# A one-core transformer kernel: paced first transfers, two weight slabs by halves, five matmuls ahead, and a last norm divided anew between engines

## The reference, cut to what matters

```python
def first_block(x, g_mix, w_in, ...):
    h = _rmsnorm(x, g_mix[layer])
    proj = jnp.einsum('bsd,de->bse', h, w_in[layer])     # 1024 -> 3072
    ...
def second_block(x, ..., final_norm):
    ...
        h = h + swiglu(rmsnorm(h, ffn_norm[l]), w_gate[l], w_up[l], w_down[l])
    return rmsnorm(h, final_norm)

def rmsnorm(x, g):
    xf = x.astype(jnp.float32)
    inv = lax.rsqrt(jnp.mean(xf * xf, axis=-1, keepdims=True) + RMS_EPS)
    return (xf * inv).astype(x.dtype) * g
```

## Time and profile before

| What | Value |
|---|---|
| Median of three runs | 1027.2 us (1026.72 to 1028.21) |
| The profiled execution's own time | 1030.3 us |
| Its span, first to last instruction | 1028.6 us |
| PE busy | 1009.0 us, 98% |
| DVE, ACT, POOL busy | 707.9, 603.1, 54.7 us |
| First matmul starts | 9.07 us |
| Last matmul ends | 1021.37 us |
| Granted TensorE clock, mean | 0.997 |

### The profile page before, as it was taken

The page is one execution under the profiler, slowest core; times in us unless marked ns, Lnnn a source line. Parts: engine busy times, 40 slices in busy tenths (PEclk is TensorE's granted clock), DMA queues, the critical chain, the costliest instruction groups (busy, mean ns, idle before and its releaser), DMA issues.

```text
span 1028.6 us, 19877 instructions
## 1 busy us (share of the span) xinstructions
PE 1009.0 (98%) x7312; PEld 937.1 (91%) x7312; DVE 707.9 (69%) x1342; ACT 603.1 (59%) x1070; POOL 54.7 (5%) x76
## 2 busy tenths in 40 slices
PE   6999999999999999999999999999999999999997
PEld 6999899999999999999999999999999899999996
DVE  4645887786666668666496666668877686666664
ACT  5566786475555556555475555558655675555554
POOL 2022000030000002000020000002100020000000
PEclk9999999999999999999999999999999999999999
DMA  8643344455555554333545555554653445555531
GB/s 329 222 144 124 123 145 164 165 185 184 184 184 184 186 187 170 126 129 124 164 152 188 185 186 185 186 184 164 209 171 114 126 150 194 185 184 184 184 123 41
DMA packets 49208, 172.74 MB, mean 168 GB/s; under 512 B 5376, under 2 KB 7680, under 8 KB 49024
## 3 DMA queue, kind: packets, MB, share of 16 engines
q1 hardware_dynamic: 48096, 170.93, 50.9%
q10 hardware_dynamic: 1056, 1.05, 0.5%
HBM read 169.86 MB, written 1.05 MB: 166 GB/s over the span
## 4 chain that ended last, share of the span: by engine, by line
PE 90%; DVE 7%; ACT 2%; DMA 1%; issue 0%; POOLq 0%; SPq 0%; POOL 0%; ACTq 0%; DVEq 0%
PE bank L319 88%; DVE w_lo L1195 2%; DVE a_pair L1207 2%; PE bank L506 1%; DVE xT L1224 1%; DMA xT<-xT_dram 1%; DVE arena_r L1207 1%; ACT w_hi L814 0%; DVE tmp L1188 0%; DVE arena L1188 0%; ACT a_pair L854 0%; ACT L1027 0%; DVE arena L1498 0%; ACT soft_p L904 0%; DVE tmp L1393 0%
## 5 line engine op out<-in xcount | busy, mean ns | idle before, releaser
L319 PE MATMUL bank<-a_pair,w_hi 128*128 128x256 f32 (+1 forms) x1992 | 541.3, 344 | 9.5 <-ACT a_pair L1041 9.1
L319 PE MATMUL bank<-a_pair,w_lo 128*128 128x256 f32 x1488 | 418.2, 282 | 0.0
L814 ACT ACTIVATE w_hi<-stage 128x1024 fp32r<-128x1024 f32 x319 | 335.5, 1056 | 137.5 <-PE bank L319 132.7
L1195 DVE TENSOR_TENSOR w_lo<-stage,w_hi 128x1024 fp32r<-128x1024 f32 x319 | 390.0, 1230 | 10.5 <-ACT w_hi L814 10.3
L319 PEld LDWEIGHTS bank<-a_pair,w_hi 128*128 128x128 f32 x1992 | 344.6, 191 | 57.6 <-issue 12.6
L319 PE MATMUL bank<-arena_r,w_hi 128*128 128x256 f32 x1840 | 338.1, 285 | 1.1 <-DVE arena_r L1207 0.7
L319 PEld LDWEIGHTS bank<-arena_r,w_hi 128*128 128x128 f32 x1840 | 286.0, 191 | 5.5 <-DVE arena_r L1195 1.3
L319 PEld LDWEIGHTS bank<-a_pair,w_lo 128*128 128x128 f32 x1488 | 283.8, 191 | 0.0
L319 PE MATMUL bank<-arena_r,w_lo 128*128 128x256 f32 x920 | 259.4, 283 | 0.0
L319 PEld LDWEIGHTS bank<-arena_r,w_lo 128*128 128x128 f32 x920 | 175.5, 191 | 0.0
L1369 DVE TENSOR_TENSOR tmp<-bank,arena 128x256 f32<-128x256 f32 x123 | 51.6, 420 | 160.5 <-ACT arena L980 160.5
(11 more groups left out here) (148 smaller groups left out, 635.1 us busy)
## 6 DMA issues: line engine op xcount, KB each, us to landing
stage<-slab_dram SPq DMA_DIRECT2D x319, 512.0 KB, 4.0
con<-con_dram SPq DMA_DIRECT2D x1, 1153.5 KB, 11.6
xT<-xT_dram SPq DMA_DIRECT2D x4, 256.0 KB, 6.9
arena<-arena ACTq DMA_DIRECT2D x2, 512.0 KB, 7.3
out_dram<-arena SPq DMA_DIRECT2D x8, 128.0 KB, 2.0
vec<-vec_dram SPq DMA_DIRECT2D x1, 245.5 KB, 3.9
pos<-pos_dram SPq DMA_DIRECT2D x1, 128.0 KB, 11.5
```

The lines of the kernel that those rows point to most:

```text
L319: return nc.tensor.matmul(out, lhsT, rhs, start=start, stop=True, skip_group_check=True)
L814: nc.scalar.activation(w_hi[:, slot, :], stage[:, slot, :], ACT.Copy).then_inc(hi_made, 1)
L1195: return nc.vector.tensor_tensor(out, a, hi.bitcast(f32), ALU.subtract)
```

## The change

At the start SP issues first halves, quarters and gains, and waits between them for earlier ones to land; slabs 0 and 1 come, are split and are multiplied in halves; `vec` is cut in two, the gains (128 x 64) early and the rest behind `con`; five float32 matmuls on a tile that POOL has set to zero stand ahead of the first product on PE; the lambda work on DVE keeps its place behind `w_lo` of slab 3 and waits for the second part of `vec`; `norm_sum(0)` and what follows from it stand one slab later. At the end DVE adds the squares of chunks 0 to 4 into one tile (four additions), so that PE has four float32 matmuls and not eight; DVE makes six of the eight chunks times gain, ACT two; DVE multiplies by `rB` in four pairs of chunks; three transfers carry a pair each, and the last pair goes as two chunks, one from SP and one from ACT. POOL has no part in it.

```diff
+HALF = SLAB // 2
+WARM = 5
...
@@ sync
-            for n in range(SLOTS):
+            half_in(0, False)
+            x_in(0)
+            sp.dma_start(vec[:, 0:V_BGATE], vec_d[:, 0:V_BGATE]).then_inc(in_gain, 16)
+            x_in(1)
+            sp.wait_ge(in_half[0], 16)
+            half_in(0, True)
+            x_in(2)
+            sp.wait_ge(in_x[0], 16)
+            x_in(3)
+            sp.wait_ge(in_x[1], 16)
+            half_in(1, False)
+            half_in(1, True)
+            sp.wait_ge(in_x[2], 16)
+            first_load(2)
+            sp.wait_ge(in_x[3], 16)
+            first_load(3)
+            sp.wait_ge(loaded[1], 16)
+            first_load(4)
+            first_load(5)
+            sp.dma_start(con[:, :], con_d).then_inc(in_con, 16)
+            sp.dma_start(vec[:, V_BGATE:], vec_d[:, V_BGATE:]).then_inc(in_vec, 16)
+            sp.dma_start(pos[:, :], pos_d).then_inc(in_pos, 16)
...
-            for c in range(NC):
-                if c in POOL_CHUNKS:
-                    sp.wait_ge(pout_ready, POOL_CHUNKS.index(c) + 1)
...
+            for c in (0, 2, 4):
+                sp.wait_ge(out_ready, c // 2 + 1)
+                sp.dma_start(out_d[:, c:c + 2, :], outT[:, c:c + 2, :]).then_inc(out_done, 16)
+            sp.wait_ge(out_ready, 4)
+            sp.dma_start(out_d[:, 6, :], outT[:, 6, :]).then_inc(out_done, 16)
@@ tensor
+            pe.wait_ge(warm_ready, 1)
+            for _ in range(WARM):
+                mm(half(7, 0), soft_t[:, 0, 0:P], soft_t[:, 0, 0:TOK], True)
...
-                    if n == 3:
+                    if n == 4:
                         norm_sum(0)
...
-            for c in range(NC):
+            pe.wait_ge(ff_made, 22 * 3)
+            pe.wait_ge(fin_added, 4)
+            mm(half(7, 0), ones, sumsq[:, :], True)
+            for c in (5, 6, 7):
                 pe.wait_ge(fin_squared, c + 1)
...
+                last = mm(half(7, 0), ones, squared[:, c, :], False)
@@ scalar
+            half_split_hi(0, False)
+            act.wait_ge(in_gain, 16)
             for c in range(NC):
                 if c % 2 == 0:
                     act.wait_ge(in_x[c // 2], 16)
                 nc.scalar.activation(a_hi[:, c, :], xT[:, c, :], ACT.Copy, scale=gain(0, c)).then_inc(ahi_ready, 1)
-            for n, cs in ((1, (0, 1)), (2, (2, 3, 4)), (3, (5, 6, 7)), (4, ()), (5, ())):
+                if c == 3:
+                    half_split_hi(0, True)
+            half_split_hi(1, False)
+            half_split_hi(1, True)
+            for n, cs in ((2, (0, 1, 2)), (3, (3, 4)), (4, (5, 6)), (5, (7,))):
                 split_hi(n, n, 0)
                 squares(0, cs)
...
+            norm_end(6)
+            act.wait_ge(out_ready, 4)
+            nc.scalar.dma_start(out_d[:, NC - 1, :], outT[:, NC - 1, :]).then_inc(out_done, 16)
@@ vector
+            half_split_lo(0, False)
+            for c in range(NC):
+                dve.wait_ge(ahi_ready, c + 1)
+                scaled_lo(a_lo[:, c, :], xT[:, c, :], gain(0, c), a_hi[:, c, :]).then_inc(alo_ready, 1)
+                if c == 3:
+                    half_split_lo(0, True)
+            half_split_lo(1, False)
+            half_split_lo(1, True)
+            for n in range(2, SLOTS - LAG):
+                split_lo(n, n)
             dve.wait_ge(in_vec, 16)
...
+            for c in range(NC):
+                residual(6, c, NSLAB - 1)
+                if c == 5:
+                    for i in (1, 2, 3, 4):
+                        add_square(i)
+            for c in range(2, NC):
+                dve.wait_ge(x_ready, 8 * 5 + c + 1)
+                nc.vector.tensor_scalar(gained[:, c, :], xT[:, c, :], gain(6, c), None, ALU.mult).then_inc(fin_made, 1)
+            dve.wait_ge(fin_made, NC)
             dve.wait_ge(r_ready, 7)
...
+            for c in range(0, NC, 2):
+                times(outT[:, c:c + 2, :], gained[:, c:c + 2, :], rB[:, :].unsqueeze(1).to_broadcast([P, 2, TOK])
+                      ).then_inc(out_ready, 1)
@@ gpsimd
+            nc.gpsimd.memset(soft_t[:, 0, 0:TOK], 0.0).then_inc(warm_ready, 1)
```

More of the change, by code:

```diff
@@ L163, in trunk @@
         in_x = [sem(f"in_x{i}") for i in range(4)]
-        in_vec, in_con, in_pos, out_done = (sem(n) for n in ("in_vec", "in_con", "in_pos", "out_done"))
+        in_gain, in_vec, in_con, in_pos, out_done = (sem(n) for n in ("in_gain", "in_vec", "in_con", "in_pos", "out_done"))
+        in_half, half_hi, half_lo = ([sem(f"{n}{i}") for i in range(2)] for n in ("in_half", "half_hi", "half_lo"))
+        warm_ready = sem("warm_ready")
         loaded = [sem(f"loaded{i}") for i in range(SLOTS)]
@@ L269, in _, with x_in, half_in, first_load @@
         def _(sp):
-            for n in range(SLOTS):
-                sp.dma_start(stage[:, n, :], slab_d[n]).then_inc(loaded[n], 16)
-                if n == 0:
-                    sp.dma_start(vec[:, :], vec_d).then_inc(in_vec, 16)
-                    for i in range(4):
-                        sp.dma_start(xT[:, 2 * i:2 * i + 2, :], xT_d[:, 2 * i:2 * i + 2, :]).then_inc(in_x[i], 16)
-                if n == 4:
-                    sp.dma_start(con[:, :], con_d).then_inc(in_con, 16)
-                    sp.dma_start(pos[:, :], pos_d).then_inc(in_pos, 16)
+            def x_in(i):
+                sp.dma_start(xT[:, 2 * i:2 * i + 2, :], xT_d[:, 2 * i:2 * i + 2, :]).then_inc(in_x[i], 16)
+            def half_in(n, second):
+                if second:
+                    sp.dma_start(stage[:, n, HALF:SLAB], slab_d[n, :, HALF:SLAB]).then_inc(loaded[n], 16)
+                else:
+                    sp.dma_start(stage[:, n, 0:HALF], slab_d[n, :, 0:HALF]).then_inc(in_half[n], 16)
+            def first_load(n):
+                sp.dma_start(stage[:, n, :], slab_d[n]).then_inc(loaded[n], 16)
+            half_in(0, False)
[20 more added lines that the diff above has]
+            sp.dma_start(pos[:, :], pos_d).then_inc(in_pos, 16)
             def load(n, at):
@@ L344, in first_column_slabs @@
                 for k in range(NC + 1):
+                    if n == 0 and k == 0:
+                        pe.wait_ge(half_lo[0], 1)
+                    if n == 0 and k == NC // 2:
+                        pe.wait_ge(lo_made, 1)
                     if k < NC:
@@ L356, in column_slab @@
             def column_slab(n, slot, out, hi=a_hi, lo=a_lo, kv=False):
-                pe.wait_ge(lo_made, n + 1)
+                if n == 1:
+                    pe.wait_ge(half_lo[1], 1)
+                else:
+                    pe.wait_ge(lo_made, n + 1)
                 for k in range(NC):
+                    if n == 1 and k == NC // 2:
+                        pe.wait_ge(lo_made, n + 1)
                     if kv:
@@ L1169, in _ @@
                 act.wait_ge(x_ready, 8 * 5 + c + 1)
-                nc.scalar.activation(squared[:, c, :], xT[:, c, :], ACT.Square).then_inc(fin_squared, 1)
-            for c in range(NC):
-                nc.scalar.activation(gained[:, c, :], xT[:, c, :], ACT.Copy, scale=gain(6, c)).then_inc(fin_made, 1)
-                if c == 1:
-                    norm_end(6)
+                nc.scalar.activation(squared[:, c, :] if c else sumsq[:, :], xT[:, c, :], ACT.Square
+                                     ).then_inc(fin_squared, 1)
+                if c == 3:
+                    for i in range(2):
+                        nc.scalar.activation(gained[:, i, :], xT[:, i, :], ACT.Copy, scale=gain(6, i)
+                                             ).then_inc(fin_made, 1)
+            norm_end(6)
+            act.wait_ge(out_ready, 4)
+            nc.scalar.dma_start(out_d[:, NC - 1, :], outT[:, NC - 1, :]).then_inc(out_done, 16)
         @block.vector
```

76 lines of the change are left out of this document (38 added, 38 removed).

## The result

The changed kernel took 1032.07 us (median of five runs, 1031.00 to 1032.62), beside 1027.2 for the kernel before: ratio 1.0031, interval [1.0016, 1.0046]. It is slower by 0.3%, where 4.1 us less were forecast. Two more measurements agree: the same kernel once more, 1.0022 [1.0010, 1.0035], and its start alone with the end of before, 1.0025 [1.0013, 1.0036]. The profiled execution took 1032.07 us, its span 1030.0.

The account below looks back on a forecast made before the run. PE was taken to bound the kernel, leaving only start and end to win: 2.9 us plus 1.2 us, 4.1 us off the median of 1027.2, giving 1023.1 us, range 1020.9 to 1025.8.

Parts of the forecast that it names:

- What bounds the kernel: Whole kernel: PE works 1009.0 of 1028.6 us, so only its waits, the start and the end can be won.
- the stretch near 411 us: Granted clock 0.50 for some 3.4 us, worth 1.5 us; the result moves if only one kernel's runs show it.
- First data: Start: half of slab 0 lands at about 3.5 us, x's second quarter at 5.3, first product at about 5.2.
- the slow stretch: Start, 4.30 to 6.00 us: transfers moved only 200 GB/s; if it recurs, landings come up to 2 us later.
- the sum: Start: slab 3 ends at 18.4 us, slab 4 is ready at 20.2 against 23.10 before, 2.9 us won.
- The five matmuls: PE ahead of the first product: they raise the clock early, so 2.6 us of half clock lie ahead of 9.95.
- The wait moved to DVE's lambda work: Start: vectors land at 17.8 us (16.6 to 19.5), hold DVE's `w_lo`, and slab 4 is ready at 20.2.
- The rule that I set against the change: Start transfers: coalesce many small transfers into a large one; cutting slabs and waiting between them should lose bandwidth.
- Rival 3: Start: paced transfers are slow, vectors at 22.5, slab 4 at 25, 1.9 us lost, 1.2 won at end: 1027.9; 6%.
- The mark: Start: the event both kernels share, PE ending slab 3 and going on with slab 4, at 23.10 us before.
- The end: Last norm and output: float32 matmuls 0.3 us earlier, last issue 1.6 earlier; 1.2 us won, bounds 0.2 and 1.6.

Follow-up runs that it names:

- e10: Changed kernel without SP's six waits, with the lambda work behind three more `w_lo`, and without the five matmuls on the cleared tile: 1028.43 us, 0.9995 of before.
- e16: Changed kernel without SP's six waits and with the lambda work moved behind three more `w_lo`, a repeat of an earlier run: 1028.83 us, 0.9996 of before.
- e1: Changed kernel's start with the last norm and output of the kernel before: 1031.93 us, 1.0025 of before.
- e9: The changed kernel once more, nothing altered: 1030.54 us, 1.0022 of before.
- e14: Changed kernel with SP's six waits at the start taken away and nothing else: 1028.90 us, 1.0003 of before.
- e15: Changed kernel, waits kept, second part of `vec` issued ahead of slabs 4 and 5; repeat of e12: 1028.96 us, 1.0002 of before.
- e13: Changed kernel with the second part of `vec` issued ahead of slab 4 and no six waits on SP: 1029.02 us, 0.9997 of before.
- e4: The kernel before once more, unchanged, as control and for a second profile: 1.0001.
- e2: The start of the kernel before with the changed last norm and output: 1029.09 us, 1.0003 of before.
- e12: Changed kernel, waits kept, second part of `vec` issued ahead of slabs 4 and 5: 1028.63 us, 1.0003 of before.

## Why the prediction was wrong

**What bounds the kernel** was read rightly: nothing from slab 6 to the last feed-forward round changed, but for the stretch near 411 us, which comes and goes in every kernel.

**First data.** Right in its steps: `w_hi` of the first half from 3.56, the first product at 5.75 (5 to 6 forecast). x's second quarter landed at 6.8 and not 5.3, in the slow stretch that the prediction allowed up to 2 us for. SP's queue then passed this on, because slab 1's first half waits for that quarter: slab 1 began at 11.65 against 9.95. PE waited 0.58 us more for slab 2 and ended slab 3 at 21.4, where the sum had 18.4.

**The five matmuls.** The clock rose in slab 0, as forecast: products of slab 0 are 0.21 us apart up to 6.75 and 0.12 from 7.57 on, and slabs 1 to 3 ran at 0.12 us per matmul. But the 2.6 us counted for it were not won: e10 without them and e16 with them are level. The profiles suggest why: a faster PE waits for slabs, where at half pace it came late enough not to.

**The wait moved to DVE's lambda work: this is the step that failed.** Place and mechanism were right to the engine: DVE idle with `vec` as releaser, `w_lo` of slab 4 queued behind, PE idle 1.93 us ahead of slab 4 (1 to 2.5 forecast), nothing after it. The size was not. The vectors, put at 17.8 with 19.5 as the bound, came at 21.2 in the changed kernel's profile, 20.9 in e1's and 21.3 in e9's. I carried 418 GB/s, which the earlier trace rows show for a queue filled with no waits, over to one with six waits; it moved 275 and 336 up to 15 us and 351 on the whole. By the windows 1.69 MB had moved by 8.30, not 1.93, and the 5.63 MB were reached at about 19.7, not 15.9 to 17.15. The landing followed 1.5 us later, between the 0.7 and 2.3 of the prediction (slab 0 alone bears out the 0.7: by windows of the kernel before its 0.52 MB had moved by about 3.6 us, and it landed at 4.3). And I chose 17.8 with the argument that pacing leaves less in the queues. It does shorten each transfer (`con` 8.9 us against 11.6 in the earlier trace rows, x 4.2 against 6.9), but `con` was issued at 11.75 and not at 6.6. Time in the queue had only been moved to SP's wait. From 17.8 to 21.2 are 3.4 us. The lambda work took 0.4 and not 0.98 us, but `w_lo` 1.6 and not 1.4, so slab 4 started 3.1 us later than the 20.2 of the sum, and the 2.9 us won were gone. Not all of it is the vectors': PE itself was free only at 21.4, so with the vectors on time 1.2 of the 3.1 us would have been lost all the same, to slabs 1 and 2, which stand behind the same waits and came late; 1.9 are the vectors'. e14 takes away the waits alone (vectors at 19.7, level with before), e15 moves the vectors alone (at 15.1, level with before).

The rule that I set against the change was the Trainium skill's on coalescing (DMA: Bandwidth & Descriptors, Rules for kernel authors). That row gives 64 KB as the size under which overhead is most of the cost; the halves here are 256 KB. Runs with the same cut transfers and no waits moved 408 and 412 GB/s (e14, e13), so here it was not the cutting. The same table of the Trainium skill says, for overlapping transfers with compute, to issue a transfer early and wait for its semaphore late. The six waits do the reverse on SP. The row names the fixed setup cost as what is hidden by it and nothing on rate; what the traces add is 351 against 408 GB/s with the waits as the only difference.

**Rival 3** had this mechanism and was given 6%. It put the vectors at 22.5 and said "slower by over 0.2% once the vectors land beyond 24". They came at 21.2 and the kernel was slower by 0.2 to 0.3%: its point of decision counted 1.2 us from the end and took the earlier trace rows's 23.10 as the mark. Both were off.

**What the prediction didn't price.** A wait of nearly 2 us on PE can be followed by a stretch at half clock: in the changed kernel's profile 3.4 us from about 24.4 on, some 1.4 us of time. e1 and e9 lose without it. I had priced PE's idle time ahead of the first matmul this way, and not the new wait that I forecast.

**The mark.** The profile of before was a late draw: slab 6 at 30.11, where the three others with that start have 28.3 to 29.2. x landed from 8.3 us on there and from 5.8 on in e4's, whose first matmul started at 6.76 and not 9.07. The gain was reckoned against an x that is late in some executions only. Against the average of the four, 28.98, that is 1.1 us of the forecast.

**The end.** Each step came out smaller. PE: 0.07 us won, not 0.3, since the four additions took 2.00 us (1.84 in the sum) and PE waited for them 1.42. Last issue: 1.2 and not 1.6. The output was moved faster, in 3.1 us at 338 GB/s (330 taken), but its transfers land in 2.2 to 2.6 us after issue (2.0 to 2.1 before) and 0.4 us came on outside the span. 1.2 was forecast; about 0.2 is what the profile leaves, and e2 measures 1.0003.

**The misses in sum**, for the profiled execution: 3.1 us at slab 4, 1.4 for the stretch at half clock, 1.1 for the mark and 1.0 at the end are 6.6. Between 4.1 us forecast as won and 2.3 to 3.2 measured as lost lie 6.4 to 7.3. It is one execution's account; e1 and e9, without the stretch, lost 1.3 to 1.4 us at slab 6 against the average and still measured 2.3 to 2.6 us slower, so about 1 us of their loss is not seen in these two starts.

**What stays open.** e12, e15, e13 and e16 reach slab 6 some 0.6 to 1.8 us ahead of the old start's average, and are level in time. The four starts of before that were profiled may be later than its usual ones, or the difference lies in the spread near 411 us; the runs can't tell. None of the repaired kernels is shown to beat the kernel before by 0.2%. Why waits between issues lower the rate is open too: the runs show that they do, and until when.

## What to carry to other kernels

A wait placed in a queue that issues transfers delays everything behind it: reckon the last needed piece from when it will be issued, with a rate measured under the same waits, not from a queue that was never empty. When a transfer is moved back, look for the first instruction that waits for it and what stands behind that on its engine; here a small transfer early, or the waiting work later, cost nothing that could be measured. And take the mark from several profiles: an idle stretch at the start that depends on one landing is a draw, and the gain from removing it is no larger than its average.
